# The additions of a norm's result to the residual, shared between GpSimd and VectorE

## The reference

```python
def rms_norm(x, w):
    y = xf * lax.rsqrt(jnp.mean(xf * xf, axis=-1, keepdims=True) + NORM_EPS)
    return (y * w).astype(x.dtype)

    # first_block
    mix = jnp.concatenate([y_ret, y_nsa], axis=-1) @ w_out[l]
    x = x + rms_norm(mix, norm_mix_post[l])                       # site 1
    h = rms_norm(x, norm_ffn_pre[l])
    x = x + rms_norm(conv_ffn(h, ...), norm_ffn_post[l])          # site 2
    return x
    # second_block begins with
    x = x + ab_mixer(rms_norm_2(x, ab_norm[j]), ...)
```

## Time and profile before

| what | us |
|---|---|
| median of three executions | 2193.11 |
| profiled execution, own time | 2191.74 |
| its span, first to last instruction | 2190.0 |
| TensorE busy | 1977.3 (90%) |
| VectorE busy | 1176.3 (54%) |
| ScalarE busy | 733.2 (33%) |
| GpSimd busy | 64.2 (3%) |

### The profile page before, as it was taken

One profiled execution on the slowest core, in us unless ns is written; L12 is line 12 of the kernel. 1 busy time (PEld: TensorE's weight loads), 2 busy tenths in 40 slices (PEclk: granted clock), 3 DMA queues, 4 the chain that ended last, 5 costly groups with the idle time before them and its releaser, 6 DMA issues.

```text
span 2190.0 us, 24671 instructions
## 1 busy us (share of the span) xinstructions
PE 1977.3 (90%) x8864; PEld 1568.7 (72%) x8864; DVE 1176.3 (54%) x1687; ACT 733.2 (33%) x1036; POOL 64.2 (3%) x63
## 2 busy tenths in 40 slices
PE   4897799889999987877799999996699999999997
PEld 3786577678888765665588888885466668888886
DVE  4566654575664667846554434455456635343444
ACT  3335222342332344323242323331334434232232
POOL 1020000200000020000000000000000000000000
PEclk9999799899999988998899999998799999999998
DMA  4224102222323331220023333332111112333333
GB/s 149 75 73 131 36 1 79 65 82 91 97 96 96 96 97 62 81 65 19 18 88 96 96 96 96 97 99 66 39 39 39 48 49 87 97 98 98 97 99 107
DMA packets 48325, 172.06 MB, mean 79 GB/s; under 512 B 5168, under 2 KB 5168, under 8 KB 48112
## 3 DMA queue, kind: packets, MB, share of 16 engines
q1 hardware_dynamic: 45504, 163.60, 24.0%
q10 hardware_dynamic: 2736, 7.32, 0.9%
HBM read 168.80 MB, written 2.10 MB: 78 GB/s over the span
## 4 chain that ended last, share of the span: by engine, by line
PE 31%; issue 17%; DVE 3%; ACT 1%; POOL 0%; POOLq 0%; ACTq 0%; DVEq 0%
PE ps L417 8%; PE ps L419 8%; PE ps L418 8%; PE ps L625 3%; PE ps L599 1%; PE ps L616 1%; DVE h_lo L1566 0%; PE ps L460 0%; ACT osbb L1198 0%; PE ps L477 0%; PE ps L634 0%; PE ps L856 0%; ACT w_hi L1004 0%; DVE w_lo L1479 0%; DVE y L1541 0%
## 5 line engine op out<-in xcount | busy, mean ns | idle before, releaser
L1004 ACT ACTIVATE w_hi<-raw 128x1024 fp32r<-128x1024 f32 x305 | 322.9, 1060 | 943.7 <-PE ps L419 942.9
L417 PE MATMUL ps<-h_hi,w_hi 128*128 128x512 f32 (+1 forms) x1376 | 552.9, 402 | 57.2 <-DVE w_lo L1479 35.4
L418 PE MATMUL ps<-h_lo,w_hi 128*128 128x512 f32 (+1 forms) x1376 | 542.1, 394 | 0.0
L419 PE MATMUL ps<-h_hi,w_lo 128*128 128x512 f32 (+1 forms) x1376 | 541.8, 394 | 0.0
L1479 DVE TENSOR_TENSOR w_lo<-raw,w_hi 128x1024 fp32r<-128x1024 f32 x305 | 373.3, 1226 | 216.1 <-ACT w_hi L1004 207.0
L417 PEld LDWEIGHTS ps<-h_hi,w_hi 128*128 128x128 f32 (+1 forms) x1376 | 262.1, 190 | 126.4 <-DVE w_lo L1479 35.6
L419 PEld LDWEIGHTS ps<-h_hi,w_lo 128*128 128x128 f32 (+1 forms) x1376 | 261.4, 190 | 56.8
L418 PEld LDWEIGHTS ps<-h_lo,w_hi 128*128 128x128 f32 (+1 forms) x1376 | 262.1, 190 | 55.8 <-issue 2.2
L417 PE MATMUL ps<-hid_hi,w_hi 128*128 128x512 f32 x688 | 268.6, 390 | 5.6 <-DVE hid_lo L1952 5.6
L418 PE MATMUL ps<-hid_lo,w_hi 128*128 128x512 f32 x688 | 268.4, 390 | 0.0
L419 PE MATMUL ps<-hid_hi,w_lo 128*128 128x512 f32 x688 | 268.3, 390 | 0.0
(11 more groups left out here) (347 smaller groups left out, 2296.7 us busy)
## 6 DMA issues: line engine op xcount, KB each, us to landing
raw<-in_panels SPq DMA_DIRECT2D x308, 512.0 KB, 3.6
x_in<-in_x ACTq DMA_DIRECT2D x1, 2048.0 KB, 16.7
x<-in_x ACTq DMA_DIRECT2D x1, 2048.0 KB, 8.6
out<-y SPq DMA_DIRECT2D x8, 256.0 KB, 2.1
first<-in_first ACTq DMA_DIRECT2D x1, 1568.0 KB, 19.9
second<-in_second ACTq DMA_DIRECT2D x1, 768.0 KB, 4.2
small<-in_small ACTq DMA_DIRECT2D x1, 332.0 KB, 5.2
masks<-in_masks ACTq DMA_DIRECT2D x1, 256.0 KB, 6.9
```

Of the source, the lines that this page charges most:

```text
L417: nc.tensor.matmul(out, a[0], b[0], start=start, stop=False)
L418: nc.tensor.matmul(out, a[0], b[1], start=False, stop=False)
L419: return nc.tensor.matmul(out, a[1], b[0], start=False, stop=stop)
L1004: nc.scalar.activation(w_hi[:, panel % 2, :], raw[:, panel % 4, :], ACT.Copy).then_inc(w_hi_ready, 1)
```

## The change

GpSimd adds only the even tiles 0, 2, 4 and 6 and counts them in `x_ready`. VectorE adds the odd tiles itself, right after it has scaled them, and counts them in a new semaphore `x_odd_ready`. ScalarE waits for the one or the other by the tile's parity. In `norm_add` scaled k for odd k is now issued with a wait for its own completion, the addition follows, with a wait for its completion as well (`signal`'s default), and `carry_low` k-2 comes behind both. Even k keeps its wait for GpSimd's addition k-2; for odd k none is needed, since VectorE itself has read that half of `tmp`.

```diff
+    x_odd_ready = sem("x_odd_ready")
@@ gpsimd
-            for k in range(KD):
+            for k in range(0, KD, 2):
                 pool.wait_ge(normed, NORMED_BEFORE[post] + k + 1)
                 nc.gpsimd.tensor_tensor(x[:, k, :], x[:, k, :], tmp[:, k % 2, :], ALU.add).then_inc(x_ready, 1)
@@ scalar, added_carry
             for k in range(KD):
-                act.wait_ge(x_ready, added + k + 1)
+                ready = (x_odd_ready if k % 2 else x_ready, (added + k) // 2 + 1)
+                act.wait_ge(*ready)
                 carry_high(name, k)
-                square(name, k, x_ready, added + k + 1)
+                square(name, k, *ready)
@@ vector, norm_add
             for k in range(KD):
-                if k >= 2:
-                    dve.wait_ge(x_ready, added + k - 1)
-                scaled(name, k, wait=False)
+                if k >= 2 and k % 2 == 0:
+                    dve.wait_ge(x_ready, (added + k) // 2)
+                scaled(name, k, wait=k % 2 == 1)
+                if k % 2:
+                    signal(V.tensor_tensor(x[:, k, :], x[:, k, :], tmp[:, 1, :], ALU.add), x_odd_ready)
                 if k >= 2:
                     carry_low(following, k - 2)
             carry_low(following, KD - 2)
             carry_low(following, KD - 1)
```

## The result

The change makes the kernel slower by 4.4 us: medians of twenty executions each are 2196.72 us (2194.65 to 2200.45) after and 2192.32 us (2190.83 to 2194.0) before, ratio 1.0019 with a 95% interval of 1.0013 to 1.0025, which is 2.9 to 5.5 us. The forecast was +2.5 us and 2195.6 us, with a range of 2191.8 to 2198.8 us, which holds the measured time.

A forecast was written before the change was run, and what follows sets the result against it. At the sites VectorE and GpSimd are full and TensorE's slow start paces most; +1.5 us at site 1 and +1.0 at site 2 on 2193.11 gave 2195.6 us, range 2191.8 to 2198.8.

The forecast's parts named there:

- The bound: At both sites GpSimd and VectorE are full, but TensorE's slow start paces most; GpSimd's relief alone is worth nothing.
- The lock: VectorE operations with two SBUF inputs wait until 0.2 us before GpSimd's addition ends; GpSimd ends 1.13 after VectorE's release.
- The late tile: In dense_two, TensorE idles some 1.0 us before tile 5; +1.5 us at site 1, +1.0 at site 2.
- (a): Rival at the sites: no lock on VectorE's additions, only +0.8 us, 2193.9 us; chance 15%.
- (b): Rival at the sites: GpSimd's addition starts just ahead of carry_low, additions held longer; +6, 2199.1 us; chance 8%.
- (d): Rival at the sites: faster, GpSimd's chain paces; TensorE loses its 0.3 us wait at tile 6, 2192.8 us; chance 6%.
- (c): Rival in dense_two: new TensorE idle time halves the granted clock from tile 5, 3.6 us per site, 2202.8 us; chance 4%.
- Any delay of the end of `dense_two` is thus passed on whole: After each site, the next panel waits for dense_two's last matmul, so the sites' +1.5 and +1.0 us reach the total.
- the lower bound: Low end of the whole-time range, 2191.8 us: +0.8 less the 1.5 us over which three executions spread.

The follow-up runs named there:

- odd_left_out: Changed kernel with the odd tiles' additions left out altogether, nobody adds them; 2193.99 us, ratio 1.0005 to the kernel before.
- before_busy: Kernel before, with eleven and sixteen matmuls into an unused PSUM bank where TensorE idles ahead of dense_two, both sites; 2195.44 us, ratio 1.0013.
- tiles_1_7_busy: VectorE adds only tiles 1 and 7, from PSUM, plus eleven and sixteen filler matmuls ahead of dense_two; 2192.15 us, ratio 1.0006 to the kernel before.
- odd_in_psum: Changed kernel, but odd scaled results go to a free PSUM bank, from which VectorE's addition reads them; 2192.73 us, ratio 1.0000 to the kernel before.
- site1_only: Kernel before with the change made at site 1 alone; 2196.47 us, ratio 1.0022 to the kernel before.
- site2_only: Kernel before with the change made at site 2 alone; 2197.87 us, ratio 1.0022 to the kernel before.
- late_tile_5: Kernel before with three additions into scratch ahead of carry_low 5 at both sites; 2200.88 us, ratio 1.0036 to the kernel before.
- tiles_1_7: Changed kernel, but VectorE adds only tiles 1 and 7, from PSUM, carry_low 5 ahead of addition 7; 2193.92 us, ratio 1.0009 to the kernel before.

## Why the prediction came out as it did

- The bound: right for this kernel. TensorE's slow start paces the sites and GpSimd's chain doesn't, as odd_left_out shows with its gain of 0.5 and 0.1 us. The margin is small, though: before_busy and tiles_1_7_busy show that behind the slow start the pace of `h_lo` comes next, within 0.1 us at site 1 and 0.3 at site 2.
- The lock: right. That GpSimd holds up VectorE's addition is shown by odd_in_psum. The other direction is read from rows: GpSimd's addition at 409.30 ends at 411.02, 1.14 behind the end of `carry_low` 0 (409.88), where I had 1.13. The additions took 1.20, 1.00, 1.01 and 1.02 us where I had 1.07, 0.85, 0.95 and 0.95. They were longer since VectorE is let in 0.14 us before GpSimd's end, not 0.2, and since it asks earlier: a self-wait leaves 0.03 us (407.21 to 407.24) where I had 0.10. The two errors cancel in the end of the site, which is luck. Against an operation without a wait, which starts 0.07 early, it costs 0.10; so of the Trainium skill's rule ("VectorE: DVE Perf Modes", section "The DRAIN you can't avoid"), that a semaphore between chained operations is free, these rows show a small exception.
- The late tile: right. Tile 5 starts 14.24 us behind scaled 0 (420.04 - 405.80) where I had 14.26, and the sites lose 1.47 + 1.08 = 2.55 us, forecast 2.5. Rivals (a), (b) and (d) fall with that, and (c) as I had it: the clock doesn't fall inside `dense_two`. But what I held against (c), that the clock stays at 1.00 behind 1.81 us of idle time, isn't so in the changed kernel: behind the same 1.81 us it is at half from 426.8 us on, at a price of 1.5 us instead of the 3.6 of (c).
- What failed is the step from the sites to the whole: "Any delay of the end of `dense_two` is thus passed on whole". It is passed on, but a stretch at half clock is added behind site 1 (+1.48), and less clock is lost behind site 2 (-1.14), together +0.3. Another 0.46 us lies outside of the span: the time less the span is 2.20 to 2.30 us in every execution of the changed kernel, and 1.74 to 1.84 of the kernel before. I hadn't looked there.
- 2.55 + 0.34 + 0.46 is 3.35 us, inside of the interval of 2.9 to 5.5. That the absolute forecast, 2195.6, is only 1.1 us off 2196.72 while the difference is 1.9 off is luck too: the three executions it started from had a median 0.8 us above that of twenty. And the lower bound, by its own terms (2193.11 + 0.8 - 1.5), is 2192.4, not 2191.8; nothing hangs on it here. The rest up to 4.4 isn't placed. Profiles of kernels that don't differ ahead of site 1 reach it between 402.46 and 405.80 us, the late ones with half-clock stretches near 100 and 205 us. Whether the changed kernel has these more often stays open.
- Also open: what brings the loss of some 5 us between 970 and 1100 us, seen in the profiles of site1_only, site2_only and late_tile_5; executions 4 us and more above the median are rare in the kernel before (4 of 119 above 2196 us) and common in site2_only, late_tile_5 and tiles_1_7. And open is why the time outside of the span is 2.25 us in six of the thirteen kernels and 1.8 in the others. The three additions of scratch alone didn't bring the latter.

## What to carry to other kernels

Moving an operation off a "slow" engine can pay only if the engine that takes it has room in that very stretch: here VectorE had none in ten microseconds, and GpSimd's unbroken 12.70 us, with ScalarE waiting behind each addition, looked like the bound while TensorE's slow start hid it. Ask which consumer waits for what is queued behind the moved operation; putting `carry_low` ahead of the addition gave back 0.9 us a site, and an input in PSUM instead of SBUF gave back 1.3, both for free. And where the matrix clock changes often, differences of a few microseconds in the whole time don't measure a site: measure between two events of the site in the trace, where the changed sites repeated to 0.02 us.

## What was not expected of the hardware

A shift of 1 to 2 us of the later work changes where the granted clock is half, far from the change: +1.5 to +1.8 us directly behind site 1 in all five profiles in which site 1 ended over 1 us late and the wait behind it was left idle, in none of the six others without matmuls filled in, -1.1 us around 936 us in the profiles of the changed kernel, and up to +7 us behind site 2. Filling one idle stretch moved the loss rather than removing it. The time outside of the span takes one of two values, 1.8 or 2.25 us, fixed for a kernel over all its executions.
